# The final layer norm of a one-core transformer kernel: eight tile buffers become rings of three, and the normalization moves from VectorE to ScalarE

## The reference, cut to what matters

```
def _layernorm(x, w=None, b=None, eps=LN_EPS):   # (x - mean) * rsqrt(var + eps), then * w + b
...
f = _moe_ffn(h.reshape(-1, D_MODEL), *moe_w).reshape(h.shape)
x = _layernorm(DN_ALPHA * x + g2 * f, ln2_w[l], ln2_b[l])
return x
```

## Time and profile before

| | before |
|---|---|
| times of 3 runs | 4913.12, 4906.5, 4909.55 us |
| median | 4909.55 us |
| profiled execution: own time, span | 4913.12 us, 4911.2 us |
| span: start of this stage's first load | 4859.58 us |
| span: start of the last store | 4908.40 us |
| VectorE busy in 4850 to 4912 us | 42.73 us |
| ScalarE busy in 4850 to 4912 us | 2.90 us |

### The profile page before, as it was taken

The page is one execution under the profiler, slowest core; times in us unless marked ns, Lnnn a source line. Parts: engine busy times, 40 slices in busy tenths (PEclk is TensorE's granted clock), DMA queues, the critical chain, the costliest instruction groups (busy, mean ns, idle before and its releaser), DMA issues. The chain is left out here.

```text
span 4911.2 us, 68803 instructions
## 1 busy us (share of the span) xinstructions
PE 4282.7 (87%) x28006; PEld 2486.3 (51%) x28006; DVE 1999.0 (41%) x4080; ACT 1334.3 (27%) x3093; POOL 519.0 (11%) x560
## 2 busy tenths in 40 slices
PE   5999689999997899999997754888698799999993
PEld 2455456654444566444546643777586344434341
DVE  1631556622714566232005567666435422212124
ACT  2111545511014555111013354333122111111110
POOL 0000000000000000000000000222100522232320
PEclk9999879999998999999998775888797899999997
DMA  5011000030111001421111011000203388999994
GB/s 189 22 59 43 31 18 14 12 148 20 45 58 40 9 14 64 182 86 43 67 63 47 1 37 65 3 3 3 87 26 124 154 272 294 318 311 331 337 330 148
DMA packets 152451, 505.37 MB, mean 103 GB/s; under 512 B 22609, under 2 KB 79554, under 8 KB 138690
## 3 DMA queue, kind: packets, MB, share of 16 engines
q1 hardware_dynamic: 114898, 379.89, 20.7%
q0 software_dynamic: 37232, 120.99, 8.9%
HBM read 402.42 MB, written 98.42 MB: 102 GB/s over the span
## 5 line engine op out<-in xcount | busy, mean ns | idle before, releaser
L697 PE MATMUL banks<-arena 128*128 128x512 f32 (+1 forms) x2928 | 1108.5, 540 | 15.2 <-DMA arena<-in_w_in 9.5
L697 PEld LDWEIGHTS banks<-arena 128*128 128x128 f32 x2928 | 560.3, 192 | 562.3 <-issue 522.4
L3125 PE MATMUL banks<-arena 128*32 128x512 f32 (+2 forms) x2896 | 561.2, 595 | 3.1 <-DMA arena<-in_experts 2.3
L884 PE MATMUL banks<-arena 128*128 128x256 f32 (+1 forms) x1152 | 377.8, 483 | 20.1 <-DMA arena<-y_d 14.3
L1248 PE MATMUL banks<-arena 96*128 96x512 f32 (+1 forms) x800 | 376.7, 554 | 11.8 <-ACT arena L1351 10.1
L3125 PEld LDWEIGHTS banks<-arena 128*32 128x32 f32 (+2 forms) x2896 | 198.7, 130 | 356.6 <-issue 353.9
L1298 DVE TENSOR_REDUCE arena<-banks 128x1 f32<-128x512 f32 (+1 forms) x400 | 238.3, 596 | 241.7 <-PE banks L1248 240.2
L884 PEld LDWEIGHTS banks<-arena 128*128 128x128 f32 x1152 | 222.3, 194 | 167.0 <-issue 147.9
L3144 PE MATMUL banks<-arena 128*32 128x512 f32 (+2 forms) x1448 | 286.4, 595 | 1.7 <-DVE arena L3174 1.2
L1256 PEld LDWEIGHTS banks<-arena 128*128 128x128 f32 x1312 | 171.6, 143 | 153.7 <-issue 123.0
L3092 POOL DMA_INDIRECT r_d<-arena x125 | 181.5, 1452 | 639.0 <-DVE arena L3174 530.3
(11 more groups left out here) (503 smaller groups left out, 5724.3 us busy)
## 6 DMA issues: line engine op xcount, KB each, us to landing
arena<-in_experts SPq DMA_DIRECT2D x64, 3072.0 KB, 13.0
arena<-in_ada_w SPq DMA_DIRECT2D x12, 2048.0 KB, 7.7
arena<-in_w_in SPq DMA_DIRECT2D x19, 1024.0 KB, 5.8
arena<-in_w_mod SPq DMA_DIRECT2D x8, 2048.0 KB, 17.9
arena<-in_w_in SPq DMA_DIRECT2D x7, 2048.0 KB, 9.4
arena<-in_w_out SPq DMA_DIRECT2D x6, 2048.0 KB, 10.6
arena<-in_w_mod SPq DMA_DIRECT2D x8, 1024.0 KB, 5.1
arena<-r_d SPq DMA_DIRECT2D x16, 512.0 KB, 11.4
```

What stands on the lines that cost most here:

```text
L697: i = e.matmul(self.out_of(n), lhs, rhs, start=k == 0, stop=k == KT - 1)
L884: i = e.matmul(bank(n % 4)[:, 0:nn], w[:, q, :], H[:, q, t0:t0 + nn], start=q == 0, stop=q == KT - 1)
L3125: op = e.matmul(ABK[(q - q0) % 2][rows, :], xT[(q - q0) % 2][:, P * k:P * k + P][:, rows], weights[:, i % SLOTS, 512 * k:512 * k + 512], s ...
```

## The change

The buffers `rr` and `r1` become rings of three, with tile i in buffer i modulo 3. A third ring of three, `rs`, takes the normalized tile. The loads of tiles 0, 1 and 2 are issued at once. The loads of tile i from 3 on are issued after the store of tile i-3, and wait for "done" of tile i-3. Stores leave from `rs`.

VectorE no longer subtracts the mean and scales by the deviation over the whole tile. A new function `scale(i)` works on one column: the inverse of the deviation, and minus the mean times that inverse (`nb`). ScalarE then makes the normalized tile with one activation over 128x1024, `Identity(scale * x + bias)`, from `rr` into `rs`. `last(i)` on VectorE becomes two tensor by tensor instructions, times w and plus b. The order on VectorE becomes `stats(i)`, `scale(i-1)`, `last(i-2)`; on ScalarE it is the root of tile i, then the activation of tile i-1, from tile 3 on after a wait for the store of the tile three before it.

```
--- before.py
+++ after.py
@@ -3256,37 +3256,40 @@
             rest_tensor(pe), rest_vector(dve), rest_scalar(act), rest_gpsimd(pool), rest_sync(sp)
 
         low = Bump(0)
-        rr, r1 = ([low(1024) for _ in range(8)] for _ in range(2))
+        rr, r1, rs = ([low(1024) for _ in range(3)] for _ in range(3))
         w2r, b2r = low(1024), low(1024)
-        bs, mv, sd = low(12), low(16), low(8)
+        bs, mv, sd, nb = low(12), low(16), low(8), low(8)
 
         def end_sync(e):
             Tn, Vn, Sn, Gn = points("end")
 
             def rows(i):
+                if i >= 3:
+                    e.wait_ge(*Vn.at("done", i - 3))
                 for n, half in enumerate((rr, r1)):
                     ld.turn(e)
-                    e.dma_start(half[i], r_d[n][P * i:P * i + P, :]).then_inc(ld.hit("end", "r", n, i), 16)
+                    e.dma_start(half[i % 3], r_d[n][P * i:P * i + P, :]).then_inc(ld.hit("end", "r", n, i), 16)
 
             rows(0), rows(1)
             row_bcast(e, w2r, A["ln2_w_2"][0], "end", "w")
             row_bcast(e, b2r, A["ln2_b_2"][0], "end", "b")
-            for i in range(2, 8):
-                rows(i)
+            rows(2)
             for i in range(8):
                 e.wait_ge(*Vn.at("done", i))
                 ld.turn(e)
-                e.dma_start(out[0][P * i:P * i + P, :], r1[i]).then_inc(ld.hit("end", "out", i), 16)
+                e.dma_start(out[0][P * i:P * i + P, :], rs[i % 3]).then_inc(ld.hit("end", "out", i), 16)
+                if i + 3 < 8:
+                    rows(i + 3)
 
         def end_vector(e):
 
             Tn, Vn, Sn, Gn = points("end")
 
             def stats(i):
-                r = rr[i]
+                r = rr[i % 3]
                 e.wait_ge(*ld.at("end", "r", 0, i))
                 e.wait_ge(*ld.at("end", "r", 1, i))
-                e.tensor_tensor(r, r, r1[i], ALU.add).then_inc(Vn.hit(), 1)
+                e.tensor_tensor(r, r, r1[i % 3], ALU.add).then_inc(Vn.hit(), 1)
                 e.wait_ge(*Vn.own())
                 for q in range(2):
                     e.bn_stats(bs[:, 6 * q:6 * q + 6], r[:, 512 * q:512 * q + 512]).then_inc(Vn.hit(), 1)
@@ -3294,28 +3297,42 @@
                 e.bn_aggr(mv[:, 2 * i:2 * i + 2], bs).then_inc(Vn.hit(), 1)
                 e.wait_ge(*Vn.own())
                 e.tensor_scalar(sd[:, i:i + 1], mv[:, 2 * i + 1:2 * i + 2], 1.0, 1e-5, ALU.mult, ALU.add).then_inc(Vn.hit("var", i), 1)
+
+            def scale(i):
+                e.wait_ge(*Sn.at("root", i))
+                e.reciprocal(sd[:, i:i + 1], sd[:, i:i + 1]).then_inc(Vn.hit(), 1)
+                e.wait_ge(*Vn.own())
+                e.scalar_tensor_tensor(nb[:, i:i + 1], mv[:, 2 * i:2 * i + 1], -1.0, sd[:, i:i + 1], ALU.mult, ALU.mult).then_inc(Vn.hit("scale", i), 1)
 
             def last(i):
                 if i == 0:
                     e.wait_ge(*ld.at("end", "w"))
                     e.wait_ge(*ld.at("end", "b"))
-                e.wait_ge(*Sn.at("root", i))
-                e.reciprocal(sd[:, i:i + 1], sd[:, i:i + 1]).then_inc(Vn.hit(), 1)
-                e.scalar_tensor_tensor(r1[i], rr[i], mv[:, 2 * i:2 * i + 1], w2r, ALU.subtract, ALU.mult).then_inc(Vn.hit(), 1)
-                e.wait_ge(*Vn.own())
-                e.scalar_tensor_tensor(r1[i], r1[i], sd[:, i:i + 1], b2r, ALU.mult, ALU.add).then_inc(Vn.hit("done", i), 1)
-
+                e.wait_ge(*Sn.at("normed", i))
+                e.tensor_tensor(rs[i % 3], rs[i % 3], w2r, ALU.mult).then_inc(Vn.hit(), 1)
+                e.wait_ge(*Vn.own())
+                e.tensor_tensor(rs[i % 3], rs[i % 3], b2r, ALU.add).then_inc(Vn.hit("done", i), 1)
+
+            for i in range(10):
+                if i < 8:
+                    stats(i)
+                if 1 <= i < 9:
+                    scale(i - 1)
+                if i >= 2:
+                    last(i - 2)
+
+        def end_scalar(e):
+            Tn, Vn, Sn, Gn = points("end")
             for i in range(9):
                 if i < 8:
-                    stats(i)
+                    e.wait_ge(*Vn.at("var", i))
+                    e.activation(sd[:, i:i + 1], sd[:, i:i + 1], ACT.Sqrt).then_inc(Sn.hit("root", i), 1)
                 if i:
-                    last(i - 1)
-
-        def end_scalar(e):
-            Tn, Vn, Sn, Gn = points("end")
-            for i in range(8):
-                e.wait_ge(*Vn.at("var", i))
-                e.activation(sd[:, i:i + 1], sd[:, i:i + 1], ACT.Sqrt).then_inc(Sn.hit("root", i), 1)
+                    p = i - 1
+                    e.wait_ge(*Vn.at("scale", p))
+                    if p >= 3:
+                        e.wait_ge(*ld.at("end", "out", p - 3))
+                    e.activation(rs[p % 3], rr[p % 3], ACT.Identity, bias=nb[:, p:p + 1], scale=sd[:, p:p + 1]).then_inc(Sn.hit("normed", p), 1)
 
         end_sync(sp), end_vector(dve), end_scalar(act)
         gate()
```

## The result

| | times, median (lowest to highest) | ratio of the two, 95% interval |
|---|---|---|
| before | 4901.56 us (4894.83 to 4913.12, 7 runs) | |
| after | 4933.44 us (4925.58 to 4942.27, 7 runs) | 1.0069 (1.0054 to 1.0085) |

The kernel became 0.69% slower, 33.8 us on before's median (26.5 to 41.7 by the interval), where 31.2 us were forecast. The forecast of 4941 us stood on a median of 4909.55; with more runs that median fell by 8.0 us, and the measured time lies 7.6 under the forecast for that reason, 1.4 us above the lower end of the range. The profiled execution of the changed kernel took 4966.66 us and isn't one of the seven: of the 53.5 us that it took more than before's, 17.5 lie ahead of the stage that was changed.

What follows compares the result with a forecast made beforehand. VectorE was taken as the bound, at 5.46 us a tile with loads running ahead. Five round trips, 29.0 us, and 2.2 for the rest made 31.2 us, on the median of 4909.55 a forecast of 4941 us, range 4932 to 4951.

Steps and rivals of the forecast that it cites:

- add to "done" on VectorE: One tile's instructions on VectorE, from its add to its last addition: 5.64 us after the change.
- ScalarE's activation, hidden: The new 128x1024 activation on ScalarE takes 1.13 us and costs nothing, since VectorE asks for its result later.
- table loads between root and Identity: Table changes on ScalarE: none expected; a pair would add 2 x 1.28 us, hidden except about 1 us near the end.
- tile 2's add after the first load's start: Tile 2's second load lands as before, at 4871.7 us, so VectorE waits 1.1 us for it.
- round trips: Tiles 3 to 7: stats(i) waits from "done" to the loads' landing, five times 5.8 us, 29.0 in all.
- "done" of tile 5 to the last "done": The end of VectorE's list, scale(7), last(6) and last(7): 5.1 us.
- the whole: Whole change: 31.2 us slower, 29.0 from five waits for loads and 2.2 from the rest.
- The mechanism: On VectorE stats(i) directly follows the last() that frees its buffer, so tiles 3 to 7 wait for loads, 29.0 us.
- The rival by which three buffers cover the loads: Loads issued a beat ahead, only one wait for them paid: 8 us, 4918 us, within 0.2%; chance 0.04.
- What VectorE gains: VectorE's work per tile: no gain; by itself the new arithmetic would add 0.1 to 0.2 us a tile.
- R: Time from "done" to the landing of the next loads in tiles 3 to 7: 5.8 us, ends 4.7 and 7.2.
- The dearer-round-trip rival: Loads of tiles 3 to 7 land 7.2 us after "done", 7 us more in all, 4948 us; chance 0.07.

Runs made afterwards that it cites:

- e5: Changed kernel with last(i-2) ahead of stats(i) on VectorE, rings, waits and SyncE's list kept; stage 60.8 us, ratio 1.0033.
- e3: Changed kernel with rings of four for the two loaded arrays, loads of tile i waiting for "done" of tile i-4; stage 53.6 to 53.9 us not distinguished: 53.9, ratio 1.0008.
- e9: Changed kernel, loads of tile i waiting for ScalarE's activation of tile i-3 and issued ahead of the store of tile i-4; stage 52.2 us, ratio 1.0013.
- e4: Changed kernel with eight buffers for each loaded array and all loads at once; stage 52.4 us, ratio 1.0001.
- e12: Changed kernel with tile i's loads issued at "done" of tile i-3 and that tile's store held until both landed; stage 77.1 us, no ratio.
- e7: Changed kernel without the second array's load from tile 3 on, its buffer used again as it is; stage 74.9 us, no ratio.
- e8: Changed kernel with eight buffers for all three arrays, TensorE adding the two arrays into PSUM and GpSimd adding b; stage 48.9 us, ratio 1.0013.
- e10: e4 with only the addition of b moved from VectorE to GpSimd; stage 49.5 us, ratio 1.0006.
- e1: Changed kernel with the two loads of tile i issued ahead of the store of tile i-3, the wait for "done" kept; stage 83.6 us, ratio 1.0078.

## Why the prediction was right, and where its sizes were off

| step | forecast | trace after |
|---|---|---|
| add to "done" on VectorE | 5.64 us | 5.64 us |
| ScalarE's activation, hidden | 1.13 us | 1.24 us, no wait of VectorE for it |
| table loads between root and Identity | none | none |
| tile 2's add after the first load's start | 12.1 us | 13.2 us |
| round trips | 5 x 5.8 us | 5 x 6.55 us |
| "done" of tile 5 to the last "done" | 5.1 us | 5.06 us |
| the whole | +31.2 us | +36.0 us in the stage, +33.8 in the times |

**The mechanism** was the one forecast: stats(i) directly behind the instruction that frees its buffer. It is shown, not only argued: e5 changes nothing but that order; every wait for a load behind the first is gone, and 24.0 of the 36.0 us with them; e3 puts a beat between and takes 30.9; e9 releases earlier, with the same three buffers, and takes 32.6. The rival by which three buffers cover the loads fell, but it is true of other orders.

**What VectorE gains** was nothing, as forecast: e4's beat is 5.54 us against 5.46.

**The term that was mis-sized** is the round trip, 0.75 us short each time, 3.7 in all. I had 0.8 us to the first byte, 1.57 MB at 415 GB/s in 3.79, and 0.5 to 1.8 behind the last byte, and took a value inside. The stretches after show all but 16 KB of the bytes from about 4909.2 to 4913.9, 4.7 us, or 1.57 / 4.7 = 334 GB/s, and some 0.8 us from there to the landing. So it was the bytes that were put 0.9 us too low, and the time behind them was within my bounds. I had the slowness of loads in hand but in the wrong place: I read the remainder of the single loads as 1.8 us behind the last byte. In e12, where two loads move alone, their bytes run from about 4908.4 to 4911.8, 3.4 us where 415 GB/s would take 2.53, and the add starts 0.6 us behind the last of them. The price lies where the loads begin, and a store ahead doesn't take it away. The other 1.1 us is tile 2: I kept its landing from before, 12.1 us after the first load's start. In this run its add started at 13.2, and in the eight other runs in which it waited for its load between 13.0 and 13.9 (13.9 in e4, with the loads in before's order). The reason for the difference is open.

**What was luck.** The times rose by 33.8 us, close to the 31.2 forecast, but their interval of 26.5 to 41.7 can't tell one size of R from the next; the stage, which can, rose by 36.0.

The dearer-round-trip rival had 7.2; the truth lay between it and the forecast. Why the second load costs 2.06 us and not 1.26 stays open; e7 also spares its issue, some 0.4 us, and no run separates the two.

## What to carry to other kernels

A ring's depth says nothing by itself. Write down the consumer's list and find the instruction that frees the buffer: what stands between it and the first use of the refill has to last as long as the whole round trip, here 6.5 us for 1 MB behind a 0.5 MB store. A pipeline step put on one side and a buffer taken away on the other were each nearly free, 3.6 and 3.1 us, and cost 36 together. If buffers must be few, let the last reader free them and check that no other wait on the issuing queue stands ahead of the loads. And moving a factor out of a VectorE instruction that has to run anyway saves nothing.

## What the runs showed of the hardware

VectorE and GpSimd took turns. While GpSimd added two 128x1024 operands from SBUF (2.34 us), VectorE's multiplication of two SBUF operands did not start, and its 128x1 instruction with two SBUF operands, otherwise 0.16 us, took 2.33. Statistics, which read one operand, ran beside it at their usual 1.29 us, from PSUM in e8 and from SBUF in e10. The Trainium skill states this in "SBUF — State Buffer", section "Who interferes with whom": a VectorE instruction with two SBUF inputs contends with a GpSimd one that reads SBUF, one with at most one SBUF input does not, and the shared ports are an exclusive lock. The traces of e8 and e10 agree.

A transfer burst that holds loads came out slower than a running stream: 334 GB/s over 1.57 MB in the changed kernel, against 415. The engines' having been idle is not enough to explain it, since the store at the head of the same burst moved at 393 to 401 GB/s. The slow part is where loads begin: 188 to 279 GB/s for about 1 us behind the store, 131 and then 315 in e12 with loads alone, 115 to 225 for 3 us in e1 with a store issued just behind them.
